# Second placement of queries and keys: ScalarE's activations in place of SyncE's DMAs

## The reference

```
fox_attention:   q_t.k_s/8 + (c_t - c_s), causal, softmax, @ v      # 8 heads of 64, c = cumsum of log gates
diff_attention:  q.k/8 - slope*(t - s), causal, softmax, twice a head; (p1 - lam*p2) @ v   # 4 heads x 2 of 64
neighbourhood_attention: q.k/8 + rpb, masked to an 8 x 16 window of an 8 x 64 grid, softmax, @ v   # 8 heads of 64
```

## Time and profile before

| | |
|---|---|
| median of 3 runs | 1410.9 us (1409.92 to 1411.08) |
| profiled execution: span, first to last instruction | 1409.4 us (the page gives no other time of that execution) |
| busy: TensorE / VectorE / ScalarE / GpSimd | 95% / 49% / 44% / 47% |
| mean granted clock of TensorE | 0.985 of full speed |
| fox attention, about | 67 to 171 us |
| diff attention, about | 185 to 288 us |
| na attention, about | 765 to 890 us |

### The profile page before, as it was taken

One profiled execution on the slowest core, in us unless ns is written; L12 is line 12 of the kernel. 1 busy time (PEld: TensorE's weight loads), 2 busy tenths in 40 slices (PEclk: granted clock), 3 DMA queues, 4 the chain that ended last, 5 costly groups with the idle time before them and its releaser, 6 DMA issues.

```text
span 1409.4 us, 19174 instructions
## 1 busy us (share of the span) xinstructions
PE 1345.1 (95%) x6444; PEld 1114.7 (79%) x6444; DVE 691.7 (49%) x1247; ACT 614.8 (44%) x964; POOL 664.7 (47%) x884
## 2 busy tenths in 40 slices
PE   7899999789999999999989879999999999999997
PEld 5877887668888888888779668877778888888887
DVE  6477656672222222121578878666435555552111
ACT  5445555564434342343434544535344444442223
POOL 5432152254655555565455223555655545554551
PEclk9999999999999999999999989999999999999999
DMA  5322231222433332333483212322323333333331
GB/s 160 83 75 68 69 102 49 76 75 75 119 89 104 89 104 82 99 96 98 90 129 102 59 54 68 104 91 86 94 69 116 99 93 100 92 98 96 99 94 60
DMA packets 227535, 127.06 MB, mean 90 GB/s; under 512 B 15972, under 2 KB 223217, under 8 KB 227473
## 3 DMA queue, kind: packets, MB, share of 16 engines
q1 hardware_dynamic: 226960, 126.04, 32.5%
q10 hardware_dynamic: 513, 0.21, 0.1%
HBM read 117.56 MB, written 2.31 MB: 85 GB/s over the span
## 4 chain that ended last, share of the span: by engine, by line
PE 82%; DVE 8%; issue 4%; DMA 3%; ACT 2%; POOL 1%; ACTq 0%; SPq 0%; DVEq 0%; POOLq 0%
PE PS L745 26%; PE PS L747 26%; PE PS L746 26%; DMA RAW<-in_w_in 1%; DVE PTL L1891 1%; POOL WL L717 1%; PE PS L934 1%; PE PS L910 1%; DMA RAW<-in_w_out 1%; DVE PR L1850 1%; PE PS L911 1%; DVE SQ L2047 1%; DVE SS L1615 0%; ACT WH L1168 0%; DVE NM L1856 0%
## 5 line engine op out<-in xcount | busy, mean ns | idle before, releaser
L717 POOL TENSOR_TENSOR WL<-RAW,WH 128x256 fp32r<-128x256 f32 x864 | 659.0, 794 | 713.3 <-ACT WH L1168 713.2
L745 PE MATMUL PS<-XH,WH 128*128 128x512 f32 x1072 | 424.0, 395 | 2.7 <-DVE X L1963 1.8
L1168 ACT ACTIVATE WH<-RAW 128x1024 fp32r<-128x1024 f32 (+1 forms) x220 | 229.0, 1043 | 450.8 <-PE PS L747 378.0
L747 PE MATMUL PS<-XH,WL 128*128 128x512 f32 x1072 | 418.6, 390 | 0.0
L746 PE MATMUL PS<-XL,WH 128*128 128x512 f32 x1072 | 418.3, 390 | 0.0
L745 PEld LDWEIGHTS PS<-XH,WH 128*128 128x128 f32 x1072 | 202.2, 189 | 44.3 <-DVE X L1963 2.6
L747 PEld LDWEIGHTS PS<-XH,WL 128*128 128x128 f32 x1072 | 201.6, 188 | 43.0
L746 PEld LDWEIGHTS PS<-XL,WH 128*128 128x128 f32 x1072 | 202.0, 188 | 39.5 <-issue 0.7
L745 PE MATMUL PS<-HH,WH 128*128 128x512 f32 (+1 forms) x374 | 141.0, 377 | 0.0
L747 PE MATMUL PS<-HH,WL 128*128 128x512 f32 (+1 forms) x374 | 140.8, 377 | 0.0
L746 PE MATMUL PS<-HL,WH 128*128 128x512 f32 (+1 forms) x374 | 140.8, 377 | 0.0
(11 more groups left out here) (326 smaller groups left out, 1861.9 us busy)
## 6 DMA issues: line engine op xcount, KB each, us to landing
RAW<-in_w_up SPq DMA_DIRECT2D x66, 512.0 KB, 3.8
RAW<-in_w_in SPq DMA_DIRECT2D x60, 512.0 KB, 3.9
RAW<-in_w_down SPq DMA_DIRECT2D x32, 512.0 KB, 3.7
RAW<-in_w_gate SPq DMA_DIRECT2D x22, 512.0 KB, 3.8
RAW<-in_w_out SPq DMA_DIRECT2D x16, 512.0 KB, 3.7
RAW<-in_w_down SPq DMA_DIRECT2D x16, 384.0 KB, 3.3
QB<-QA SPq DMA_DIRECT2D x24, 128.0 KB
KA<-KA SPq DMA_DIRECT2D x24, 128.0 KB
```

The costliest lines, as they stand in the source:

```text
L717: ins = pool.tensor_tensor(WL[:, s, cs], RAW[:, s % 2, cs], WH[:, s, cs].bitcast(F32), ALU.subtract)
L745: pe.matmul(out, ah, bh, start=start, stop=False)
L747: return pe.matmul(out, al, bh, start=False, stop=stop)
L1168: act.activation(WH[:, s, 0:width], RAW[:, s % 2, 0:width], ACT.Copy).then_inc(w_hi, 1)
```

## The change

ScalarE's `head_part` makes four activations in place of two: q high to QA and QB, k high to both halves of KA, with a new semaphore `head_rows_hi` for the second pair. The two DMAs of rows of each of the 24 heads are gone. The bias rows of fox heads 2 to 7 and of the eight diff heads (14 DMAs) are issued by ScalarE inside `head_part`, behind its waits and ahead of the activations. `head_rows` and `HEADS_BEFORE` are gone from SP: it no longer waits for `head_hi`. TensorE waits for `head_rows_hi`, and for `head_in` (one DMA a head) only in fox and diff. VectorE waits for `head_rows_hi` too, before it writes a tile T that a head was read from.

```diff
     def heads_in(kind, head):
-        return 16 * {"fox": 3 * (head // 2 + 1), "diff": 12 + 3 * (head // 2 + 1), "na": 24 + 2 * (head // 2 + 1)}[kind]
+        return 16 * {"fox": head // 2 + 1, "diff": 4 + head // 2 + 1}[kind]
...
-        def head_rows(kind, head):
-            e, mem = head % 2, FAM[kind]["mem"]
-            nat, oth = half_rows(e), half_rows(1 - e)
-            sp.wait_ge(head_hi, 2 * (FAM[kind]["h0"] + head) + 2)
-            sp.dma_start(mem["QB"][nat, e, :].bitcast(F32), mem["QA"][nat, e, :].bitcast(F32)).then_inc(head_in[e], 16)
-            sp.dma_start(mem["KA"][oth, e, :].bitcast(F32), mem["KA"][nat, e, :].bitcast(F32)).then_inc(head_in[e], 16)
-            if kind == "diff" or (kind == "fox" and head >= 2):
-                dst, src = bias_rows_of(kind, head)
-                sp.dma_start(dst, src).then_inc(head_in[e], 16)
...
         def load_units(lo, hi):
             for u in range(lo, hi):
-                for kind, head in HEADS_BEFORE.get(u, []):
-                    head_rows(kind, head)
...
                     pe.wait_ge(head_lo, 2 * (f["h0"] + head) + 2)
-                    pe.wait_ge(head_in[e], heads_in(kind, head))
+                    pe.wait_ge(head_rows_hi, 2 * (f["h0"] + head) + 2)
+                    if kind != "na":
+                        pe.wait_ge(head_in[e], heads_in(kind, head))
...
             if kind != "na" and f["h0"] + head >= 2 or kind == "na" and head >= 2:
                 act.wait_ge(sc_ready, f["s0"] + 4 * (head - 1))
-                act.wait_ge(head_in[e], heads_in(kind, head) - 16 * (2 if kind == "na" else 3))
-            for name, a, bias in (("QA", aq, B8[r, head // 2:head // 2 + 1]), ("KA", ak, vcol("b_in_2", 4 + head // 2)[r, :])):
+            if kind == "diff" or (kind == "fox" and head >= 2):
+                dst, src = bias_rows_of(kind, head)
+                act.dma_start(dst, src).then_inc(head_in[e], 16)
+            bq, bk = B8[r, head // 2:head // 2 + 1], vcol("b_in_2", 4 + head // 2)[r, :]
+            for name, rows, a, bias, ready in (("QA", r, aq, bq, head_hi), ("KA", r, ak, bk, head_hi),
+                                               ("QB", r, aq, bq, head_rows_hi), ("KA", oth, ak, bk, head_rows_hi)):
                 if kind == "na":
-                    ins = act.activation(f["mem"][name][r, e, :], tile_t(a)[r, :], ACT.Identity, bias=bias)
+                    ins = act.activation(f["mem"][name][rows, e, :], tile_t(a)[r, :], ACT.Identity, bias=bias)
                 else:
-                    ins = act.activation(f["mem"][name][r, e, :], tile_t(a)[r, :], ACT.Copy)
-                ins.then_inc(head_hi, 1)
+                    ins = act.activation(f["mem"][name][rows, e, :], tile_t(a)[r, :], ACT.Copy)
+                ins.then_inc(ready, 1)
...
             if done:
                 dve.wait_ge(head_lo, 2 * max(done))
+                dve.wait_ge(head_rows_hi, 2 * max(done))
```

More of the change, by code:

```diff
@@ L351, in program @@
     head_lo = sem("head_lo")
+    head_rows_hi = sem("head_rows_hi")
     head_in = [sem("head_in_even"), sem("head_in_odd")]
@@ L549, in program @@
     EVEN_DONE = 28
[L552 to L558, removed]
     PRF = PR[:, :, :].rearrange("p a b -> p (a b)")
@@ L624, in _ @@
         load_units(4, 6)
-        for head in range(2):
-            head_rows("fox", head)
         sp.wait_ge(pool_made, 1)
@@ L1224, in head_part @@
             f, e = FAM[kind], head % 2
-            r = half_rows(e)
+            r, oth = half_rows(e), half_rows(1 - e)
             aq, ak = head_tiles(kind, head)
```

## The result

The changed kernel takes 1415.15 us in the median of 20 runs, the kernel before 1409.84 (20 runs on the same chip): a ratio of 1.0037, 95% interval 1.0029 to 1.0045. It is slower by 5.3 us, more than the 2.8 us that can be told from no change. The forecast was 1412.2 with a range of 1405.5 to 1416; the result lies inside it, 0.85 us from its upper end, and "slower" had a chance of 0.24. In one session of the experiments one execution of the kernel before took 2547.39 us and one of the version with the late pair 2250.85, at a lower clock; the ratios leave both out. The profiled execution has a span of 1413.0 us (before: 1409.4), at a mean granted clock of 0.984 (before: 0.985).

The account below looks back on a forecast made before the run. TensorE, busy 95% of the 1409.4 us span, was taken as the bound. Fox +4.3, na +0.6, clock +2.5 and diff -6.1 made +1.3 us on the median 1410.9: 1412.2, range 1405.5 to 1416.

Parts of the forecast that it names:

- Diff, step 17: Differential attention, head 5: unit 27's load no longer waits, so TensorE's hole of 1.41 us before PV goes, -1.4 us.
- Diff, step 21: Differential attention, head 6: unit 28 lies ready early, so TensorE's hole shrinks from 6.45 to 2.8 us, -3.7 us.
- Diff, clock: Slow clock after diff's large hole costs 1.7 us of work in place of 2.7: -1.0 us, bounds 0 and -2.7.
- Growth of a head: `head_part` on ScalarE grows by 1.65 us in fox and diff (bias DMA 0.56, new pair 1.1), 1.3 in na.
- Fox +4.3: Fox: longer heads delay PTH or PTL; heads 2, 4, 6, 7 cost +0.7, +1.4, +1.6, +0.6, heads 3 and 5 nothing.
- Na +0.6: Neighbourhood attention: heads 2, 4, 6 cost +0.2 us each, slack 1.09 against growth 1.3; other three heads nothing.
- Clock in fox: Slower clock after fox holes of 2.5 us (1.7 in full) and 2.1 us (half of 1.7): +2.5, bounds 0 and 3.4.
- The rule against the change: Skill page: DMAs share 16 engines, whoever issues them; taken alone it strikes out diff's 6.1 us gain, making the sum +7.4.
- rival 4: Diff units 27 and 28 are late for the transfers' sake, not order: +7.4 us, 1418.3; chance 0.05.
- Rival 1: VectorE, not ScalarE, sets the fox holes; half of 4.9 goes, no clock lost: -5.4 us, 1405.5; chance 0.24.
- Rival 3: Writes from one half of the partitions to the other take 1.06 us each: about +10 us, 1421; chance 0.06.
- Rival 2: Both fox holes (steps 15, 23) count as long and diff's clock costs as before: +3.2 us, 1414.1; chance 0.15.

Follow-up runs that it names:

- the late pair: Changed kernel with the bias DMA, QB and other half of KA after the next step's PTH and exponential on ScalarE: 1402.83 us, 0.9956 against the kernel before.
- the shifted queue: Kernel before with diff's six head rows one unit later in SyncE's queue, SyncE still copying everything: 1401.27 us, ratio 0.9953.
- the run that kept the waits: Changed kernel, but SyncE still waits at the old places for `head_hi` and issues no copies: 1418.58 us, ratio 1.0051 against the kernel before.

## Why the prediction was right or wrong

The mechanism was right in both directions: late weights in diff, longer heads in front of PTH in fox and na. The sign came out as forecast and the size did not: +5.3 us for +1.3. That it stayed inside the range owes something to the range's width. The steps that failed are sizes: the growth of a head (1.65 for 1.85, in na 1.3 for 1.48), the clock behind the hole of diff (-1.0 for -0.5), and na (+0.6 for +2.5).

- **Diff, step 17 (-1.4): right.** The hole went. That the load was free of order once SyncE did not wait is shown by the shifted queue (0.9953); that it was the copies as much as the waits, by the run that kept the waits.
- **Diff, step 21 (-3.7): right in kind, 0.2 too much.** 6.45 became 2.95, not 2.8. The forecast gave it all to the waits; 1.1 us of it was the three DMAs ahead of the load. The holes of diff made -5.0 for -5.1.
- **Diff, clock (-1.0): right in kind, twice too much.** 3.4 us at 1.2 GHz after the hole in place of 6.8. The forecast priced the slow stretch of before at 2.7 us, from the mean of the eight microseconds from 252; TensorE was idle for the first of them, so 1.0 us of slow clock was charged that slowed nothing. By the shorter stretches above it cost 2.2, the new one costs 1.7, and the difference is 0.5 us (0.4 by place). Holes (-5.0), clock (-0.4) and small pauses (+0.2) make the 5.1 us, to 0.1, by which diff is shorter in the trace, in place of 6.1.
- **Growth of a head (1.65 us): mis-sized.** The four writes are spaced 0.54, 0.52, 0.64 and 0.65 us, so the new pair adds 1.3 and not 1.1; with the 0.55 us from the issue to QA it is 1.85. In na the spacings are 0.63, 0.61, 0.74 and 0.74, and the pair adds 1.48, not 1.3. The forecast took the overlap of two neighbours for granted. The Trainium skill, page "ScalarE: Activation LUTs", section "What ACT_TABLE_LOAD costs", says that back-to-back activations overlap by about 93 ns. The trace agrees where both write the natural half (0.63 long, next start after 0.54) and disagrees for the write across.
- **Fox +4.3: the holes made +4.9.** Heads 2, 4 and 6 came out at +1.03, +1.70 and +1.86 for +0.7, +1.4 and +1.6, each too small by 0.3. Head 7, priced at +0.6, cost nothing: PTL was 0.3 us late there, and TensorE had fill work to do. Head 3, priced at nothing for its slack, cost 0.4. The slack was there (PTH ended 2.3 us before PTL began), and the cost came another way: a scaling on VectorE (L1879, L1864 now), which stands ahead of that PTL, took 0.40 us longer. First before, then after:

```profile
100.11 0.36 DVE L1879 TENSOR_SCALAR PR<-PR,RI 128x256 f32<-128x256 f32 x1
```

```profile
98.92 0.76 DVE L1864 TENSOR_SCALAR PR<-PR,RI 128x256 f32<-128x256 f32 x1
```

- **Na +0.6: mis-sized, +2.5 by place.** The three heads cost 0.44 to 0.5 each for 0.2: the growth was 1.48 against a slack of 1.09. Three more holes grew by 0.14, 0.14 and 0.33, the last not shown to be the change's. The other 0.5 is clock: the slow stretch of 6.8 us near head 6 is in both traces, but after the change it begins later against the hole, so that more of it lies over work.
- **Clock in fox (+2.5): two new stretches of 3.4 us at 1.2 GHz, +2.9 by place** (1.4 and 1.5). The one counted half happened in full.
- **The rule against the change** (rival 4, freed queue brings nothing) fell. The shifted queue issues every DMA of before, from the same engine, and is 0.47% faster. The Trainium skill, "DMA: Bandwidth & Descriptors", section "Issuing engines are not separate DMA queues", says that the DMAs share their engines whoever issues them; no run here speaks against that. What was won here is the time for which a load stood behind a wait.
- **Rivals.** Rival 1 (ScalarE soaks it up) fell with the holes of 1.66 to 2.77. Rival 3 (writes across cost 1.06) fell: 0.63 us each, though its direction was right by 0.1. Rival 2, "the clock decides", has the nearest number (1414.1) and a part of the cause: both stretches in fox came, but the one in diff got shorter. Its rule, that a hole's length decides somewhere between 1.4 and 2.4 us, doesn't hold: one of 2.36 us was followed by no slow stretch (last section).

By size: by place the two profiled executions differ by +7.2 in fox (forecast 6.8 with its clock), -5.1 in diff (-6.1), +2.5 in na (0.6) and -1.0 at the start, 3.6 us in all. Without the start, which is not the change's, the stages make +4.6, so 3.3 of the miss of 4.0 us are placed: 1.9 in na, 1.0 in diff, 0.4 in fox. The other 0.7 between 4.6 and 5.3 is open; executions of the changed kernel alone spread over 6.2 us.

## What to carry to other kernels

Before moving work to another engine, ask what stands behind the old wait in its queue. Here what the change won came from a load that stood behind a wait and three DMAs in an in-order queue: of 3.5 us at the larger hole 2.4 were the wait's, and moving the wait with its DMAs by one place won at least as much (0.9953). Work that is added to an engine should go behind what the next engine waits for: in fox and na the second pairs and the issues cost 9.4 us in front of WH and PTH (1.0067), and one step later they left all seven of these holes as they were. In these runs a DMA that ScalarE issued on an idle datapath, right after a wait, cost its whole issue; behind running work it cost none. When a slow stretch of the clock is priced, only the part of it that lies over work counts: 6.8 us cost 2.2 here, 3.4 us cost 1.7.

## What the runs showed of the hardware

- An activation from one half of the partitions to the other overlaps neither neighbour: 0.64 to 0.66 us from start to start at 64 x 512, against 0.52 to 0.54 between writes within a half (with a bias: 0.74 against 0.61 to 0.63).
- An issue of a DMA of bias rows on ScalarE takes 0.48 to 0.56 us of its queue. It was paid in full (0.52 to 0.55 us of a hole) or not at all (0.00), by where it stood.
- VectorE's operations on SBUF slow down beside POOL's WL: the same 128 x 512 multiply took 1.26 us against 0.73, a 128 x 384 mask step 0.89 against 0.34. When ScalarE rounded a weight thus set how long VectorE took a microsecond later. Not every step beside WL is slowed: the scaling of 128 x 256 after head 3 of fox took 0.36 us before and 0.76 after, with POOL at WL both times.
- After like holes the clock fell for 3.4 us, for 6.8 us, or not at all. In one run (pair one step later) a hole of 2.22 us was followed by 6.8 us at 1.2 GHz, and one of 2.36 us by none (0.57 over 8 us is 6.9 us):

```profile
244.00:252.00 8.00, 7.26 (x27) 6.17 (x28) 6.72 (x17) 6.65 (x16) 2.41 (x4) 0.57 0.21 68
798.00:806.00 8.00, 5.64 (x35) 4.52 (x33) 5.72 (x15) 5.37 (x13) 3.37 (x4) 1.00 0.22 64
```

  What a slow stretch cost depended on where it began: 2.2 us for one of 6.8 that began in the hole, 1.7 for one of 3.4 that lay over work.
